# Routing stage of a two-block transformer kernel: wider router products, fewer rank products, VectorE rests in parts

## The reference

```python
g_logits = (xt @ w_rg) + b_rg                      # 4 groups
g_idx = jnp.argmax(g_logits, axis=-1)
g_w = softmax(g_logits)[g_idx]
e_logits = ((xt @ w_re) + b_re).reshape(T, 4, 8)   # only the chosen group's 8 count
e_val, e_loc = lax.top_k(e_logits[g_idx], 2)
e_w = softmax(e_val) * g_w
# each token goes through its two experts:
# hid = silu(x @ w1[e]) * (x @ w3[e]);  out += e_w * (hid @ w2[e])
```

## Time and profile before

| | |
|---|---|
| median of 3 runs | 1203.87 us |
| lowest, highest | 1202.14, 1206.37 us |
| profiled execution | 1205.15 us, span 1203.3 us |
| TensorE busy | 1149.5 us, 96% of the span |
| VectorE busy | 487.0 us, 40% |
| ScalarE busy | 409.8 us, 34% |
| GpSimd busy | 231.5 us, 19% |
| mean granted clock of TensorE | 0.984 |
| read from memory | 329.84 MB, 275 GB/s over the span |

### The profile page before, as it was taken

How to read it: one execution, slowest core, us unless ns; L and a number is a source line. 1 busy time by engine, 2 the same in 40 slices (tenths; PEclk the granted TensorE clock), 3 DMA queues, 4 the chain that set the end, 5 groups by cost and what they waited for, 6 DMA issues and landing times.

```text
span 1203.3 us, 15528 instructions
## 1 busy us (share of the span) xinstructions
PE 1149.5 (96%) x5906; PEld 762.1 (63%) x5906; DVE 487.0 (40%) x967; ACT 409.8 (34%) x607; POOL 231.5 (19%) x104
## 2 busy tenths in 40 slices
PE   4899999999999999999989988899999999999998
PEld 1578767774444444544434435888877778888886
DVE  1595552752222222222212215789454653333226
ACT  3533444232111111211112105664244363534334
POOL 0362233300000000000000003400313335442522
PEclk8899999989999999999999999999999999999999
DMA  9986366679899999999999995533213464654541
GB/s 377 342 303 247 141 225 258 270 295 377 329 389 422 422 422 422 422 422 422 422 421 422 421 420 196 210 138 135 79 71 140 149 205 145 198 153 180 203 160 50
DMA packets 89193, 331.68 MB, mean 276 GB/s; under 512 B 3873, under 2 KB 26690, under 8 KB 62514
## 3 DMA queue, kind: packets, MB, share of 16 engines
q1 hardware_dynamic: 88512, 330.36, 70.5%
q0 software_dynamic: 432, 0.48, 0.2%
q10 hardware_dynamic: 194, 0.06, 0.0%
HBM read 329.84 MB, written 1.05 MB: 275 GB/s over the span
## 4 chain that ended last, share of the span: by engine, by line
PE 74%; DMA 17%; DVE 5%; ACT 1%; issue 1%; SPq 1%; POOL 0%; DVEq 0%; ACTq 0%
DMA ring<-in_w 15%; PE ps L832 14%; PE ps L833 13%; PE ps L834 13%; PE ps L1150 13%; PE ps L1192 5%; DMA ring<-in_w_ada 2%; PE ps L1122 1%; PE ps L892 1%; PE ps L1123 1%; PE ps L1303 1%; SPq L721 1%; ACT ring_r L1502 1%; PE ps L946 1%; PE ps L944 1%
## 5 line engine op out<-in xcount | busy, mean ns | idle before, releaser
L807 POOL TENSOR_TENSOR ring_r<-ring,ring_r 128x1024 fp32r<-128x1024 f32 x80 | 207.3, 2611 | 819.2 <-ACT ring_r L1502 819.2
L1150 PE MATMUL ps<-ring,arena 128*64 128x512 f32 x1008 | 225.9, 596 | 8.6 <-DMA ring<-in_w 7.5
L833 PE MATMUL ps<-ring_r,hl_r 128*128 128x512 f32 x528 | 211.5, 400 | 0.0
L832 PE MATMUL ps<-ring_r,hl_r 128*128 128x512 f32 x480 | 197.5, 411 | 12.0 <-DVE ring_r L1924 5.1
L834 PE MATMUL ps<-ring_r,hr_r 128*128 128x512 f32 x480 | 192.5, 401 | 0.0
L1502 ACT ACTIVATE ring_r<-ring 128x2048 fp32r<-128x2048 f32 x90 | 167.2, 1907 | 63.1 <-PE ps L834 44.9
L1150 PEld LDWEIGHTS ps<-ring,arena 128*64 128x64 f32 x1008 | 69.5, 137 | 148.8 <-issue 127.6
L1924 DVE TENSOR_TENSOR ring_r<-ring,ring_r 128x2048 fp32r<-128x2048 f32 x50 | 118.3, 2373 | 92.3 <-ACT ring_r L1502 92.1
L832 PEld LDWEIGHTS ps<-ring_r,hl_r 128*128 128x128 f32 x480 | 92.0, 192 | 41.0 <-issue 18.3
L833 PEld LDWEIGHTS ps<-ring_r,hl_r 128*128 128x128 f32 x528 | 101.2, 192 | 22.3
L834 PEld LDWEIGHTS ps<-ring_r,hr_r 128*128 128x128 f32 x480 | 91.9, 191 | 22.4
(11 more groups left out here) (363 smaller groups left out, 1656.8 us busy)
## 6 DMA issues: line engine op xcount, KB each, us to landing
ring<-in_w SPq DMA_DIRECT2D x91, 2048.0 KB, 21.5
ring<-in_w_in SPq DMA_DIRECT2D x21, 2048.0 KB, 8.1
ring<-in_w_ada SPq DMA_DIRECT2D x8, 2048.0 KB, 9.0
ring<-in_w_ffn_gate SPq DMA_DIRECT2D x11, 1024.0 KB, 5.2
ring<-in_w_ffn_up SPq DMA_DIRECT2D x11, 1024.0 KB, 7.7
ring<-in_w_ffn_down SPq DMA_DIRECT2D x5, 2048.0 KB, 7.7
ring<-in_w_ada SPq DMA_DIRECT2D x8, 1024.0 KB, 10.1
ring<-in_w_o SPq DMA_DIRECT2D x2, 2048.0 KB, 7.7
```

Of the source, the lines that this page charges most:

```text
L807: nc.gpsimd.tensor_tensor(rest[:, a:b], w[:, a:b], lead[:, a:b].bitcast(F32), ALU.subtract).then_inc(sem("w_rest_b"), 1)
L832: mm(o, lhsT=a_lead, rhs=b_lead, start=start, stop=False, skip_group_check=True)
L833: mm(o, lhsT=a_lead, rhs=b_rest, start=False, stop=False, skip_group_check=True)
L1150: last = mm(H[slots_of(e), :], lhsT=xs[:, k, slots_of(e)], rhs=w, start=k == 0, stop=k == KD - 1)
```

## The change

1. `logits`: the moving operand of each product is three neighbouring blocks of the router's weights, 108 columns in place of 36. The output's place is shifted so that the wanted 36 always fall on columns 72 to 107 of the bank; the other columns hold sums that nobody reads. VectorE reads `src[:, 72:108]`.
2. `keep_x`: five ahead of the ranks and one behind, in place of six and two.
3. The ranks: three products, of 64, 64 and 32 columns, in place of five of 32.
4. Masking: `first_max` for the groups leaves a mask of the groups not chosen; one instruction for each token tile (128x32) adds -1e30 to their experts. It takes the place of three instructions (128x8, 128x64, 128x64), each linked to the next.
5. `x1_rests` for the first half of the columns is cut in two parts of 128x256 for each token tile: the first stays ahead of the reading of `rank`, the second goes behind the one-hot matrices and ahead of the maximum that releases the bank of `rank`. `gather(0)` waits for each part where it needs it, `gather(1)` for the sixth signal.

```diff
             def logits(t):
...
-                    last = mm(o[:, 0:ROUTES], lhsT=x1T[:, k, t * P:(t + 1) * P], rhs=wrs[:, k, :], start=k == 0,
-                              stop=k == KD - 1)
+                    first = min(k, KD - 3)
+                    at = (2 - k + first) * ROUTES
+                    last = mm(o[:, at:at + 3 * ROUTES], lhsT=x1T[:, k, t * P:(t + 1) * P], rhs=wrs[:, first:first + 3, :],
+                              start=k == 0, stop=k == KD - 1, skip_group_check=True)
...
-            keep_x(0, True)
             keep_x(1, True)
             o = small.claim(pe, "rank")
             pe.wait_ge(sem("cst_in"), 16)
             pe.wait_ge(sem("chosen_ready"), 1)
             chosen = rt[:, 0, :, :]
-            mm(o[:, 0:32], lhsT=before, rhs=chosen[:, 0, :], start=True, stop=True)
-            mm(o[:, 32:64], lhsT=before, rhs=chosen[:, 1, :], start=True, stop=False)
-            mm(o[:, 32:64], lhsT=ones, rhs=chosen[:, 0, :], start=False, stop=True)
-            mm(o[:, 64:96], lhsT=ones, rhs=chosen[:, 0, :], start=True, stop=False)
-            mm(o[:, 64:96], lhsT=ones, rhs=chosen[:, 1, :], start=False, stop=True).then_inc(small.done, 1)
-            keep_x(2, True)
-            keep_x(3, True)
+            mm(o[:, 0:64], lhsT=before, rhs=chosen, start=True, stop=False, skip_group_check=True)
+            mm(o[:, 32:96], lhsT=ones, rhs=chosen[:, 0:1, :].to_broadcast([P, 2, EXPERTS]), start=False, stop=False,
+               skip_group_check=True)
+            mm(o[:, 64:96], lhsT=ones, rhs=chosen[:, 1, :], start=False, stop=True,
+               skip_group_check=True).then_inc(small.done, 1)
+            keep_x(0, True)
...
-            def gather(n):
+            def gather(n, first=False):
 
                 for j in range(4):
+                    if first and j % 2 == 0:
+                        pe.wait_ge(sem("xp_rest"), 6 if n else j + 2)
...
             def first_gather(done):
                 pe.wait_ge(sem("moe_s_ready"), 4 * done + 4)
                 for n in range(2):
-                    pe.wait_ge(sem("xp_rest"), 2 * n + 2)
-                    gather(n)
+                    gather(n, True)
...
-            gsel = rt[:, 1, :, 0:GROUPS]
-            first_max(g, GROUPS, r1[:, 0, :], gsel, rt[:, 2, :, 0:GROUPS], r1[:, 1, :])
+            other = rt[:, 1, :, 0:GROUPS]
+            first_max(g, GROUPS, r1[:, 0, :], other, rt[:, 2, :, 0:GROUPS], r1[:, 1, :], ALU.not_equal)
...
-            link(v.tensor_scalar(rt[:, 2, :, 0:GROUPS], gsel, BIG, -BIG, ALU.mult, ALU.add))
...
-            link(v.tensor_tensor(by_group(rt[:, 3, :, :]), by_group(e), per_group(gsel), ALU.mult))
-            link(v.tensor_tensor(by_group(rt[:, 4, :, :]), by_group(rt[:, 3, :, :]), per_group(rt[:, 2, :, 0:GROUPS]), ALU.add))
+            for t in range(TT):
+                mark(v.scalar_tensor_tensor(rt[:, 4, t, :].rearrange("p (g n) -> p g n", g=GROUPS),
+                                            other[:, t, :].unsqueeze(2).to_broadcast([P, GROUPS, PER_GROUP]), -BIG,
+                                            e[:, t, :].rearrange("p (g n) -> p g n", g=GROUPS), ALU.mult, ALU.add))
+            settle()
...
-            def x1_rests(h):
+            def x1_rests(h, at, n):
...
-            x1_rests(0)
+            x1_rests(0, 0, 2)
             src = small.ready(dve, "rank")
...
             one_hot(0)
+            x1_rests(0, 2, 2)
             release(v.tensor_reduce(flagf[:, 0:1], src[0:1, 64:96], AX.X, ALU.max), small, "rank")
             v.tensor_scalar(flag[:, :], flagf[:, 0:1], float(CAP), None, ALU.is_gt).then_inc(sem("flag_ready"), 1)
-            x1_rests(1)
+            x1_rests(1, 0, 4)
```

More of the change, by code:

```diff
@@ L2098, in _ @@
                 src = small.ready(dve, f"lgt{t}")
-                release(v.scalar_tensor_tensor(lg[:, t, :], src[:, 0:ROUTES], rs[:, 1, t:t + 1], brx, ALU.mult, ALU.add),
+                release(v.scalar_tensor_tensor(lg[:, t, :], src[:, 2 * ROUTES:3 * ROUTES], rs[:, 1, t:t + 1], brx, ALU.mult, ALU.add),
                         small, f"lgt{t}")
@@ L2105, in wide_, with first_max @@
                 return a.unsqueeze(2).to_broadcast([P, TT, n])
-            def first_max(values, n, best, one_hot, tmp, least):
+            def first_max(values, n, best, one_hot, tmp, least, taken=ALU.is_equal):
                 link(v.tensor_reduce(best, values, AX.X, ALU.max))
@@ L2112, in first_max @@
                 link(v.tensor_reduce(least, tmp, AX.X, ALU.min))
-                link(v.tensor_tensor(one_hot, tmp, wide_(least, n), ALU.is_equal))
+                link(v.tensor_tensor(one_hot, tmp, wide_(least, n), taken))
             g, e = lg[:, :, 0:GROUPS], lg[:, :, GROUPS:]
-            gsel = rt[:, 1, :, 0:GROUPS]
-            first_max(g, GROUPS, r1[:, 0, :], gsel, rt[:, 2, :, 0:GROUPS], r1[:, 1, :])
+            other = rt[:, 1, :, 0:GROUPS]
+            first_max(g, GROUPS, r1[:, 0, :], other, rt[:, 2, :, 0:GROUPS], r1[:, 1, :], ALU.not_equal)
             v.tensor_tensor(rt[:, 7, :, 0:GROUPS], g, wide_(r1[:, 0, :], GROUPS), ALU.subtract).then_inc(sem("route_sub_ready"), 1)
-            link(v.tensor_scalar(rt[:, 2, :, 0:GROUPS], gsel, BIG, -BIG, ALU.mult, ALU.add))
             def by_group(a):
                 return a.rearrange("p t (g n) -> p t g n", g=GROUPS)
-            def per_group(a):
-                return a.unsqueeze(3).to_broadcast([P, TT, GROUPS, PER_GROUP])
-            link(v.tensor_tensor(by_group(rt[:, 3, :, :]), by_group(e), per_group(gsel), ALU.mult))
-            link(v.tensor_tensor(by_group(rt[:, 4, :, :]), by_group(rt[:, 3, :, :]), per_group(rt[:, 2, :, 0:GROUPS]), ALU.add))
+            for t in range(TT):
[3 more added lines that the diff above has]
+            settle()
             first_max(rt[:, 4, :, :], EXPERTS, r1[:, 2, :], rt[:, 1, :, :], rt[:, 3, :, :], r1[:, 1, :])
@@ L2134, in _ @@
             v.tensor_tensor(r1[:, 5, :], r1[:, 3, :], r1[:, 2, :], ALU.subtract).then_inc(sem("route_sub_ready"), 1)
-            def x1_rests(h):
+            def x1_rests(h, at, n):
                 for t in range(TT):
                     dve.wait_ge(sem("xp_ready"), 2 * h + t + 1)
-                    v.scalar_tensor_tensor(xp_r[t][:, 4 * h:4 * h + 4, :],
-                                           x[:, t, h * COL:(h + 1) * COL].rearrange("p (q j) -> p j q", j=4), rs[:, 1, t:t + 1],
-                                           xp_l[:, t, 4 * h:4 * h + 4, :].bitcast(F32), ALU.mult,
+                    blocks = slice(4 * h + at, 4 * h + at + n)
+                    v.scalar_tensor_tensor(xp_r[t][:, blocks, :],
+                                           x[:, t, h * COL:(h + 1) * COL].rearrange("p (q j) -> p j q", j=4)[:, at:at + n, :],
+                                           rs[:, 1, t:t + 1], xp_l[:, t, blocks, :].bitcast(F32), ALU.mult,
                                            ALU.subtract).then_inc(sem("xp_rest"), 1)
-            x1_rests(0)
+            x1_rests(0, 0, 2)
             src = small.ready(dve, "rank")
```

## The result

The changed kernel takes 1207.31 us (median of 6 runs, 1206.08 to 1209.31) against 1204.19 us for the kernel before (6 runs). The ratio is 1.0032, 95% interval 1.0019 to 1.0046: slower by about 3.9 us, where I had forecast 1.0 us less. It also lies above the range of the forecast, which ended at 1205.8 us.

A forecast was written before the change was run, and what follows sets the result against it. Early expert turns were taken as TensorE-bound, late ones as transfer-bound, with routing ahead counting one to one. From 1203.87 us, 2.0 us gained less 1.0 us for half clock gave 1202.9 us, range 1200.0 to 1205.8.

The forecast's parts named there:

- Gain passes one to one: Routing stage: time saved there passes whole through the transfer-bound turns to the end, for a few us.
- The sum of 3.06 - 1.05 = 2.0 us: Routing: ranks read 3.06 us earlier, less 1.05 us for the moved quarters; 2.0 us gained at full clock.
- Logits keep the clock: Logits on TensorE: 108 columns hold the full clock through them, 85 in 100.
- Clock falls in the gathers, priced at 1.0 us, recovering by 269 us: Gathers: after sparse rank work the clock halves within 262 to 269 us, losing 1.0 us (bounds 0.3 and 2.9).
- rival D: Routing: clock falls near 262 us, stays half until the first expert products; 0.9 us lost, 1204.8 us; 8 in 100.
- rival A: Whole routing: the clock stays full all along; 2.0 us gained, 1201.9 us; 25 in 100.
- Fewer copies cost nothing: Ahead of the ranks: five copies, 0.9 us each at full clock, end at 260.1 us and no longer hold the ranks.
- The release order: Ahead of the first gather: TensorE waits 1.5 us, ended by VectorE's maximum behind the moved quarters, not by a rest.

The follow-up runs named there:

- before_again: The kernel before, unedited, profiled a second time; routing 26.09 us.
- copies_as_before: The changed kernel with six copies ahead of the ranks and two behind; ratio 1.0001 to the kernel before, routing 25.91 us.
- before_third: The kernel before, unedited, profiled a third time; routing 26.10 us.
- narrow_logits: The changed kernel with logits back at 36 columns, one block per product; ratio 1.0029 to the kernel before, routing 30.40 us.
- five_and_one: The kernel before with only the copies changed, five ahead of the ranks and one behind; ratio 1.0023 to the kernel before, routing 31.42 us.
- more_copies: The changed kernel with three more copies, six ahead of the ranks and three behind; ratio 0.9985 to the kernel before, routing 25.93 us.
- release_first: The changed kernel with the maximum that releases the rank bank ahead of the moved quarters; ratio 1.0020 to the kernel before, routing 29.09 us.
- five_and_two: The changed kernel with one more copy behind the ranks, five ahead and two behind; ratio 1.0007 to the kernel before, routing 25.88 us.

## Why the prediction was wrong, point by point

**Gain passes one to one.** Right in kind. Turns after are 27.7 us (321.88 to 349.60) and 29.8 us (527.71 to 557.52), unchanged, and 2.50 of the 2.65 us lost in the routing are still there at 527 us. Single profiles don't carry it to the end: the spans differ by 1.0 us only (1203.3 and 1204.3), for each has further dips of its own. That of the earlier trace rows from 719.30 us, for one, has no counterpart in the profile after. Over the experiments, the ratios follow the routing, with about 0.1% of scatter: 29.1 to 31.4 us go with 1.0020 to 1.0032, 25.1 to 26.2 us with 0.9979 to 1.0007.

**The sum of 3.06 - 1.05 = 2.0 us: this step failed.** Its instructions were nearly right. Masking gave two records in 0.29 us (I took 0.32), the quarters have a pitch of 0.58 us (0.52), three rank products hide within them, and VectorE read the ranks within 0.05 us of where I put it. What was wrong is what it was subtracted from. I took the dip from 255 to 261.8 us, which delayed ranks in the earlier trace rows, for a property of the kernel. Two further profiles have none. Against them the sum of everything but the copies is 26.09 - 25.91 = 0.2 us. With a full clock the first gather is released by VectorE's maximum in both kernels, 14.27 us behind the mark in before_again and 14.10 in copies_as_before. Of VectorE's work ahead of it only the masking (0.4 us) went; the second quarters were moved, not removed, and cutting cost 0.2 us.

**Logits keep the clock.** Right in the traces of the change, and without value: narrow ones kept it too in before_again, before_third, narrow_logits and five_and_one. Whether wide ones lower the chance of a dip that one profile in five of the narrow kernels shows is open.

**Clock falls in the gathers, priced at 1.0 us, recovering by 269 us: this failed too, in its size.** The stretch, its cause and the place were as the prediction had them: gaps of 1.26 and 2.07 us (1.1 and 1.7 predicted), then half clock in the gathers. But I gave it the 3.4 or 6.8 us of the dips in the earlier trace rows. It lasted 10.2 us. The profile of before already had one that long, at half clock from 19.5 to 29.7 us, which I had overlooked. By more_copies it cost 2.4 us in the gathers (6.31 against 3.88) and 2.1 us in the first expert product (10.03 against 7.93 to the first w3 product), 4.5 us together. That is rival D, the other side, with its mechanism and its point of decision (half clock beyond 270.5 us); but D charged 2.9 us for it, from 2.0 gained to 0.9 lost, and I gave it 8 in 100. Even D, at 1204.8 us, lies 2.5 us below the measured median.

By the Trainium skill's rule on long idle gaps ("TensorE: Matmul & The Clock Gate", section "Why this matters for your kernels") the clock should have held, as rival A had it. The runs differ: no gap in the changed kernel is longer than 2.1 us, and in five_and_one none exceeds 1.7 us, yet the clock fell each time. Nor do shorter gaps sort the runs. In release_first they were 1.27 and 0.92 us and the clock fell; in five_and_two they were 1.25 and 1.19 us and it stayed. Between the copies ahead and the first gather TensorE had 1.77 us of products in the first of these and 2.63 us, one copy more, in the second. That more products in this stretch kept the clock is shown; by what rule it falls is not.

**Fewer copies cost nothing: the root of both.** The prediction took the sixth copy only as work ahead of the ranks, 0.9 us to save. In both further profiles of the kernel before it is not on the path, since the ranks wait for the choice (gaps of 0.79 and 0.81 us); and without the two copies the clock falls. five_and_one and copies_as_before show that this part is the whole loss.

**The release order.** The first gather did wait for the maximum behind the quarters (2.07 us, ended by L2166), as forecast. It made the stretch between copies and gather 1.15 us longer, but with the maximum first the clock fell all the same.

Not settled: why the ratios of five_and_one (1.0023, routing 5.3 us longer) and of the change (1.0032, routing 4.3 us longer) don't stand in the order of their routings. Their intervals overlap, each routing is from one or two profiles, and the dips behind the routing (3.4 or 6.8 us each, between 620 and 790 us) differ from profile to profile.

## What to carry to other kernels

Repeated products that change nothing may be there to hold TensorE's clock. Before taking one out, compare the whole stretch that is left with stretches of your own traces that kept the clock and that lost it, products and gaps, and not the longest gap alone. Price the half clock over everything up to the point where the rows show it full again; here one copy of 0.9 us stood against 4.6 us of routing.

A dip of the clock in one profile is one execution. Before it is subtracted as a gain, a second profile of the same kernel is worth more than any working; and if the dip goes, the next engine's chain (here VectorE's, which the change hardly shortened) may be the real bound.

## What the runs showed of the hardware

Once down, the clock did not come back during gathers. In the changed kernel TensorE ran 32 gather records of 128 columns end to end from 266.5 to 272.8 us, each with its own load of the stationary operand. The clock fell 0.7 us into them and stayed down; it rose at 277.5 us, 4.7 us into products of 512 columns. In release_first it rose 2.9 us into them, in narrow_logits 3.1, in five_and_one 5.0 us. Where it had not fallen, the same records ran at full clock: in more_copies and five_and_two it was 1.00 throughout the gathers. So in these profiles records that ran at a full clock without losing it did not restore it once it was gone.
